# Six modulation row tiles multiplied on VectorE during the first feed-forward stage, and two more moved into the loop over recurrent heads

## The chip, the cores and the metric

The kernel runs on one core of a Trainium2 chip. Its time is the device time of one execution in microseconds (us), the median of three runs. Engines are named as the profile names them: PE is TensorE (PEld its weight loads), DVE is VectorE, ACT is ScalarE, POOL is GpSimd, SP is the queue that issues most DMAs.

## The reference, cut to what matters

Two transformer blocks follow each other, on 256 tokens of width 1024, all in fp32. What the change touches is the first block's conditioning: nine rows of 1024 numbers, computed once from a single vector `c`, that scale, shift and gate the three sub-blocks.

```
sc = silu(c)                                         # c: (1, 1024)
mod = sc @ ada_w + ada_b                             # ada_w: (1024, 9*1024)
(sh1, sc1, g1, sh2, sc2, g2, sh3, sc3, g3) = split(mod, 9)

y = rmsnorm(h, ffn1_pre_g) * (1 + sc1) + sh1
y = (silu(y @ w_gate) * (y @ w_up)) @ w_down         # 1024 -> 2816 -> 1024
h = h + 0.5 * g1 * rmsnorm(y, ffn1_post_g)
y = rmsnorm(h, mix_pre_g) * (1 + sc2) + sh2
y = token_mix(y, ...)                                # two recurrent mixers, 4 heads each
h = h + g2 * rmsnorm(y, mix_post_g)
...                                                  # second feed-forward with sh3, sc3, g3
...                                                  # second block: attention, RWKV, 16384 experts
```

## The kernel before

All large weights come through one ring in SBUF of four slots of 1 MB (a chunk is 128 partitions x 2048 fp32 numbers). SP issues the chunks in the order in which they are consumed. It may refill a slot when PE has begun the chunk after the one in it: `begun` counts the chunks that PE has begun, and chunk g is issued at `begun >= g - 2` (L2476).

The feed-forward matmuls are fp32 split in two: ACT casts a chunk to its rounded top (`top_chunk_act`, L342, two halves of 1024 columns), DVE subtracts the top in place to leave the rest (`rest_chunk_dve`, L353, two halves), and PE does three passes (L375 to L377). The first stage has 22 gate-and-up tiles (`staying_split_pe`, 48 matmuls with 256 columns each, one chunk each) and then 11 down chunks (`down_part`). After each gate-and-up tile ACT takes the silu (L856) and DVE multiplies and splits the result (L914, L369, L370). ACT may cast tile i+1 once PE has begun tile i, since the tops have two slots. DVE does, in program order, the rest of tile i+1 and then the product of tile i (`hidden_tile`).

The rows of `mod` come in 18 tiles of 512 columns, numbered 0 to 17. Each takes two chunks of `ada_w`. Tiles 0 to 3 are made before the stage. Tile t is made on PE in three steps: `ada_groups_pe` (L641, eight fp32 matmuls with 32 weight columns and 512 moving columns, four of them side by side in the array, then the bias, L650), a copy by ACT (L661), and `ada_sum_pe` (L657), a matmul with a matrix of ones that sums the partitions and spreads the result over all of them, evacuated by ACT (L665). Tiles 4 to 9, 14 and 15 are hosted in the first stage: behind every one of its first 16 gate-and-up tiles stands half of such a tile, and so its chunk stands in the ring. Tiles 10 and 11 stand behind the stage, 12 and 13 behind the loop over recurrent heads, 16 and 17 behind the mixer's output. `ada_rest_dve` (L724) scales rows SC2 (tiles 8, 9), SC3 (tiles 14, 15) and G1 (tiles 4, 5) in the down part.

The loop over recurrent heads (L1105 on, eight iterations) makes on PE the decays of the next step (L1071 to L1076), the attention matmuls of this one (`attend`, L1087) and the read-out of the last (L1098). ACT takes the exponentials (L1181), and DVE multiplies (L1302, L1304), masks (L1313) and reduces (L1320). ACT and DVE take each of them in the same order.

Of the kernel before, what the change touches and what calls it, by code (L numbers as in the profile page):

```python
# [14 lines left out]
ALU = mybir.AluOpType  # L15
# [8 lines left out]
S, D, F = 256, 1024, 2816  # L24
# [167 lines left out]
def program(nc, dram, out, where):  # L192

    ctx = ExitStack()
    with ctx:
# [373 lines left out]

        def staying_split_pe(pe, queue):  # L570

            bank = queue.take(pe)
            w = next_split_chunk(pe, KT)
            for j in range(2):
                for k in range(KT):
                    first, last = three_passes(pe, bank[:, j * S:(j + 1) * S].rearrange("p (t s) -> p t s", t=TT),
                                               [x[:, j * P:(j + 1) * P] for x in w[k]],
                                               (y_top[:, :, k, :], y_rest[:, :, k, :]), k == 0, k == KT - 1)
                    if j == 0 and k == 0:
                        first.then_inc(begun, 1)  # L580
            last.then_inc(queue.done, 1)
# [39 lines left out]
        ADA, ADA_FIRST = N_MOD * D // 512, 4  # L621
        HOSTED = [4, 5, 6, 7, 8, 9, 14, 15]
        BEHIND = {"ffn1": (10, 11), "scan": (12, 13), "mix": (16, 17)}

        def partial(tile):

            if tile < ADA_FIRST:
                return arena3[:, tile * 512:(tile + 1) * 512]
            if tile in HOSTED:
                return arena5[:, 7 * D - 512:7 * D]  # L630
            where, at = {10: (arena3, 2048), 12: (arena3, 4096), 16: (arena2, 0)}[tile - tile % 2]
            return where[:, at + tile % 2 * 512:at + tile % 2 * 512 + 512]

        def ada_groups_pe(pe, tile, halves=(0, 1)):
            if 0 in halves:
                ada_groups_pe.bank = A.take(pe)
            bank = ada_groups_pe.bank
            for c in halves:
                w = next_chunk(pe)[:, :].rearrange("p (k n) -> p k n", k=4)
                for k in range(4):  # L640
                    ins = pe.matmul(bank[32 * k:32 * k + 32, :], silu_c[:, 4 * c + k, :], w[:, k, :],  # L641
                                    start=(c == 0), stop=(c == 1 and k > 0))
                    if k == 0:
                        ins.then_inc(begun, 1)
            if 1 not in halves:
                return

            if tile in (0, ADA_FIRST):
                pe.wait_ge(sem(f"ada_b_in{int(tile > 0)}"), 16)
            pe.matmul(bank[0:32, :], ones_32, arena1[:, tile * 512:(tile + 1) * 512], start=False, stop=True  # L650
                      ).then_inc(A.done, 1)
# [72 lines left out]
        def ada_rest_dve(dve):  # L724

            await_mark(dve, "hosted_rows")
            dve.wait_ge(sem("gains_in"), 16)
            for i, sc in ((1, SC2), (2, SC3)):
                nc.vector.scalar_tensor_tensor(mod[:, sc, :], mod[:, sc, :], 1.0, gains[:, 2 * i, :], ALU.add, ALU.mult)
            nc.vector.scalar_tensor_tensor(mod[:, G1, :], mod[:, G1, :], 0.5, gains[:, 1, :], ALU.mult, ALU.mult  # L730
# [10 lines left out]

        split_at = [4 * ADA_FIRST // 2]
        for i in range(FT + FT // 2 - 1):
            split_at.append(split_at[-1] + 1 + (i < 2 * len(HOSTED)))

# [10 lines left out]
        def ffn_pe(pe, tag):  # L756
# [43 lines left out]
            for g in range(FT // 2 - 2):  # L800
                w = next_split_chunk(pe, 2)
                for t in range(TT):
                    first = down_part(w, g, t)
                    if t == 0:
                        first.then_inc(begun, 1)
            last_two = [next_split_chunk(pe, 2), next_split_chunk(pe, 2)]
# [34 lines left out]
        def ffn_act(act, tag):  # L841
# [17 lines left out]
            if tag == "ffn1":  # L859
                for g in range(FT // 2):  # L860
                    gate(2 * g, 0)
                    if 0 < g <= len(HOSTED):
                        ada_sum_act(act, HOSTED[g - 1])
                        if g == len(HOSTED):
                            mark("hosted_rows", A.free, 4 + A.emptied.n)
                    gate(2 * g + 1, 1)
                    if g < len(HOSTED):
                        ada_groups_act(act, HOSTED[g])
                for i in range(FT + 1, FT + FT // 2 - 1):
                    top_of_tile_act(act, i)  # L870
                act.wait_ge(sem("rows_scaled"), 1)
                top_chunk_act(act, 2)
# [23 lines left out]
        def ffn_dve(dve, tag, sc, sh, g):  # L896
# [29 lines left out]
            for i in range(1, FT // 2):  # L926
                if tag == "ffn1":
                    rest_of_tile_dve(dve, FT + i)
                    if i == 1:
                        ada_rest_dve(dve)  # L930
# [87 lines left out]
        def mix_pe(pe):  # L1018
# [86 lines left out]
            for i in range(HEADS * TT):  # L1105
# [14 lines left out]
        def mix_act(act):  # L1120
# [56 lines left out]
            for i in range(HEADS * TT):  # L1177
                e = decayed[i % 2][:, 0].rearrange("p l s -> p (l s)")
                for a0, b0 in ((0, 512), (512, NL * P)) + (((NL * P, NL * P + 2 * P),) if i % TT else ()):
                    bank = A.get(act)  # L1180
                    nc.scalar.activation(e[:, a0:b0], bank[:, 0:b0 - a0], ACT.Exp).then_inc(A.free, 1)  # L1181
                mark(f"decay{i}", A.free, 4 + A.emptied.n)
            act.wait_ge(sem("h_att"), HEADS * TT)
            act.dma_start(arena2[:, 3 * D:6 * D], dram["gains"][3 * D:6 * D].partition_broadcast(P)
# [13 lines left out]
        def mix_dve(dve):  # L1198
# [146 lines left out]
            for t in range(TT):  # L1345
# [3 lines left out]
                vec.tensor_tensor(yb[:, t, :], yb[:, t, :], mixg[:, t, :], ALU.mult).then_inc(sem("y_mixed"), 1)  # L1349
            late_gate_dve(dve, G2, 1.0, 3, "ffn1")  # L1350
            residual_dve(dve, 0, G2, BY_HALF, "ffn2")
            scaled_dve(0, SC3)
# [1101 lines left out]
        source = tile_at(range(ADA_FIRST))  # L2454
        for i in range(FT):
            source.append(ffn1_at[i])
            if i < 2 * len(HOSTED):
                source.append(tile_at(HOSTED)[i])
        source += ffn1_at[FT:] + tile_at(BEHIND["ffn1"])
        source += range(rest_at, rest_at + 16)  # L2460
        source += tile_at(BEHIND["scan"]) + list(range(rest_at + 16, rest_at + 20)) + tile_at(BEHIND["mix"])
        source += range(rest_at + 20, chunk_of["mix2"])
# [5 lines left out]
        def _(sp):  # L2468
# [135 lines left out]
```

## Time and profile before

| | |
|---|---|
| median of 3 runs | 1949.12 us (1948.37 to 1952.76) |
| the profiled execution | 1958.65 us, of which its span is 1956.8 us |
| busy in the span | PE 1811.9 us (93%), DVE 1139.4 (58%), ACT 768.4 (39%), POOL 334.8 (17%) |
| chain that ended last | PE 76%, DVE 9%, DMA 7%, ACT 4% |
| mean granted TensorE clock | 0.967 of full speed |
| DMA | 315.98 MB in the span, mean 161 GB/s |

The profiled execution lies 9.5 us above the median of the runs; durations come from it alone. Busy shares are means over stages with different limits, so a stage is read by its own window. A PE row's end is modelled: a matmul of 256 columns is shown as 0.28 us while the next starts 0.12 us after it. Starts are therefore what to subtract. The first stage's gate-and-up part runs from 53.58 to 225.65 us, its down part to 290.5, the mixer to about 530, of which the loop over recurrent heads is 431 to 480.

### The profile page before, as it was taken

To read this page: it belongs to the slowest core of one execution; us is meant where nothing else is said; L and a number is where in the kernel's file an instruction comes from. 1 tells how busy PE (TensorE), PEld (TensorE's weight loads), DVE (VectorE), ACT (ScalarE), POOL (GpSimd) and SP (SyncE) were. 2 spreads that over 40 slices of the span, in tenths; PEclk is the share of its full clock that TensorE was granted. 3 is DMA by queue.
4 is the path that set the end of the run, shared out by engine and by line. 5 is a ranking of instruction groups with operands and counts; after the bars stand their busy time and mean duration, and the time that the engine had idled before them with its cause. 6 is when DMAs were issued, how large, how long until landed. Compare 5 with 4: busy or idle time off the path is not lost.

```text
span 1956.8 us, 32839 instructions
## 1 busy us (share of the span) xinstructions
PE 1811.9 (93%) x12830; PEld 1557.4 (80%) x12830; DVE 1139.4 (58%) x1952; ACT 768.4 (39%) x1170; POOL 334.8 (17%) x314
## 2 busy tenths in 40 slices
PE   4999998987899999999878899999999999999997
PEld 1777877864399978976863798999999998888885
DVE  2443545759355544695443469958889964444444
ACT  2333344451345444552111443444444443333334
POOL 1000000000000000000000038760000025555553
PEclk8999997999999998999998899999999999999999
DMA  9566554521555553442003335554444456666664
GB/s 359 208 257 245 170 178 178 185 86 66 225 172 189 176 172 119 151 151 87 3 2 129 130 123 164 179 162 140 142 141 142 145 175 192 193 192 192 193 191 158
DMA packets 62080, 315.98 MB, mean 161 GB/s; under 512 B 6896, under 2 KB 7184, under 8 KB 40720
## 3 DMA queue, kind: packets, MB, share of 16 engines
q1 hardware_dynamic: 60768, 305.94, 46.8%
q10 hardware_dynamic: 1136, 8.39, 1.2%
q8 instruction: 85, 1.39, 0.3%
q14 instruction: 27, 0.22, 0.0%
q0 software_dynamic: 64, 0.04, 0.0%
HBM read 313.29 MB, written 1.05 MB: 161 GB/s over the span
## 4 chain that ended last, share of the span: by engine, by line
PE 76%; DVE 9%; DMA 7%; ACT 4%; POOL 2%; issue 2%; SPq 0%; POOLq 0%; DVEq 0%; ACTq 0%
PE bank L375 21%; PE bank L376 20%; PE bank L377 20%; DMA ring<-in_stream 4%; PE bank L590 3%; DMA ring<-in_experts 2%; PE bank L2127 2%; DVE ring_rounded L353 2%; POOL ring_rounded L2419 2%; PE bank L536 2%; ACT arena_rounded L342 1%; PE bank L641 1%; DVE field L1320 1%; ACT ring_rounded L2225 1%; PE bank L1549 1%
## 5 line engine op out<-in xcount | busy, mean ns | idle before, releaser
L377 PE MATMUL bank<-yb_rounded,ring_rounded 128*128 128x256 f32 x2080 | 595.3, 286 | 0.0
L377 PEld LDWEIGHTS bank<-yb_rounded,ring_rounded 128*128 128x128 f32 x2080 | 406.0, 195 | 0.0
L353 DVE TENSOR_TENSOR ring_rounded<-ring,arena_rounded 128x1024 fp32r<-128x1024 f32 x218 | 256.9, 1221 | 218.7 <-ACT arena_rounded L342 218.4
L2225 ACT CAST ring_rounded<-ring 128x1024 fp32r<-128x1024 f32 x250 | 262.6, 1051 | 279.1 <-DMA ring<-in_experts 279.1
L375 PE MATMUL bank<-yb_rounded,arena_rounded 128*128 128x256 f32 x1104 | 323.5, 293 | 24.1 <-POOL ring_rounded L831 10.2
L376 PE MATMUL bank<-yT_rounded,arena_rounded 128*128 128x256 f32 x1104 | 319.7, 290 | 0.0
L342 ACT CAST arena_rounded<-ring 128x1024 fp32r<-128x1024 f32 x222 | 221.3, 1047 | 191.3 <-PE bank L375 119.6
L375 PE MATMUL bank<-yb_rounded,ring_rounded 128*128 128x256 f32 x976 | 283.0, 290 | 10.3 <-POOL ring_rounded L2419 7.9
L376 PE MATMUL bank<-yT_rounded,ring_rounded 128*128 128x256 f32 x976 | 275.9, 283 | 0.0
L2378 DVE TENSOR_TENSOR ring_rounded<-ring,ring_rounded 128x1024 fp32r<-128x1024 f32 x128 | 156.9, 1226 | 191.6 <-ACT ring_rounded L2225 191.6
L376 PE MATMUL bank<-ring_rounded,arena_rounded 128*128 128x512 f32 x688 | 268.4, 390 | 0.0
L375 PEld LDWEIGHTS bank<-yb_rounded,arena_rounded 128*128 128x128 f32 x1104 | 219.8, 199 | 40.4 <-issue 20.9
L2419 POOL TENSOR_TENSOR ring_rounded<-ring,ring_rounded 128x1024 fp32r<-128x1024 f32 x46 | 126.4, 2762 | 647.5 <-ACT ring_rounded L2225 647.5
L376 PEld LDWEIGHTS bank<-yT_rounded,arena_rounded 128*128 128x128 f32 x1104 | 219.8, 199 | 0.2 <-issue 0.2
L375 PE MATMUL bank<-ring_rounded,arena_rounded 128*128 128x512 f32 x512 | 199.4, 389 | 1.1 <-POOL arena_rounded L2437 1.1
L377 PE MATMUL bank<-ring_rounded,arena_rounded 128*128 128x512 f32 x512 | 199.2, 389 | 0.0
L375 PEld LDWEIGHTS bank<-yb_rounded,ring_rounded 128*128 128x128 f32 x976 | 186.7, 191 | 13.5 <-ACT field L2236 7.2
L376 PEld LDWEIGHTS bank<-yT_rounded,ring_rounded 128*128 128x128 f32 x976 | 186.9, 192 | 0.1
L2434 POOL CAST arena_rounded<-field 128x256 fp32r (+1 forms) x128 | 94.2, 736 | 415.7 <-PE bank L375 415.7
L376 PEld LDWEIGHTS bank<-ring_rounded,arena_rounded 128*128 128x128 f32 x688 | 129.5, 188 | 26.7
L375 PEld LDWEIGHTS bank<-ring_rounded,arena_rounded 128*128 128x128 f32 x512 | 96.1, 188 | 21.7 <-DVE ring_rounded L2378 1.5
L377 PEld LDWEIGHTS bank<-ring_rounded,arena_rounded 128*128 128x128 f32 x512 | 96.1, 188 | 20.0
(389 smaller groups left out, 2606.1 us busy)
## 6 DMA issues: line engine op xcount, KB each, us to landing
ring<-in_stream SPq DMA_DIRECT2D x160, 1024.0 KB, 4.9
ring<-in_experts SPq DMA_DIRECT2D x256, 512.0 KB, 3.5
field<-in_gains ACTq DMA_DIRECT2D x1, 2560.0 KB, 8.9
const<-in_const SPq DMA_DIRECT2D x1, 1602.0 KB, 15.1
field<-in_gains ACTq DMA_DIRECT2D x1, 1536.0 KB, 6.7
xh<-in_x ACTq DMA_DIRECT2D x1, 1024.0 KB, 5.5
field<-in_norms ACTq DMA_DIRECT2D x1, 1024.0 KB, 10.3
field<-in_lns ACTq DMA_DIRECT2D x1, 1024.0 KB, 4.7
```

The source lines that it names most:

```text
L342: nc.scalar.copy(top, ring[:, g % SLOTS, half * HALF:(half + 1) * HALF]).then_inc(sem("weight_top_ready"), 1)
L353: ins = nc.vector.tensor_tensor(ring_r[:, g % SLOTS, half], ring[:, g % SLOTS, half], top.bitcast(F32), ALU.subtract)
L375: first = pe.matmul(bank, s_top, m_top, start=start, stop=False)
L376: pe.matmul(bank, s_top, m_rest, start=False, stop=False)
L377: return first, pe.matmul(bank, s_rest, m_top, start=False, stop=stop)
L536: ins = pe.matmul(two[t][:, :], src[:, c + k, t * P:(t + 1) * P], w[:, k, :], start=(c + k == 0), stop=(c + k == k_tiles - 1))
L590: ins = pe.matmul(four[2 * t + n][:, :], yT[:, c + k, t * P:(t + 1) * P], w[:, k, :], start=(c + k == 0), stop=(c + k == KT - 1))
L2127: ins = pe.matmul(bank[:, q * P:(q + 1) * P], hot[:, g % 2, 0, q, :], hot[:, g % 2, 1, q, :], start=True, stop=True)
L2225: nc.scalar.copy(expert_top[:, n % E_SLOTS, :], expert_w[:, n % E_SLOTS, :]).then_inc(expert_top_ready, 1)
L2378: vec.tensor_tensor(expert_rest[:, slot, :], expert_w[:, slot, :], expert_top[:, slot, :].bitcast(F32), ALU.subtract).then_inc(v_split, 1)
L2419: nc.gpsimd.tensor_tensor(expert_rest[:, slot, :], expert_w[:, slot, :], expert_top[:, slot, :].bitcast(F32), ALU.subtract).then_inc(u_spl ...
L2434: nc.gpsimd.tensor_copy(h_top[:, b, :], src).then_inc(h_top_ready, 1)
```

## The change

Tiles 4 to 9 leave `ada_groups_pe`. Their ring chunks, twelve, now stand behind gate-and-up tiles 1, 3, 5, ... 21 and behind the second down chunk (`ROW_BEHIND`, numbered 1 to 23 in the joint count of both parts), one for every second tile in place of one for every tile. In `row_part_dve` DVE adds each chunk to the row in place: four `scalar_tensor_tensor` of 128 x 512, row = w * silu(c) + row, with silu(c) as a scalar per partition. The row starts as zeros with the bias in partition 0, which the prologue had already put there. Each of the four waits for the one before it. PE's part is the matmul with ones alone (`row_sum_pe`, six of them, behind joint tiles 6, 10, 14, 18, 21 and 26), and ACT evacuates it. PE passes over the row chunk, and the next tile's first matmul counts two begun chunks. SP, before it refills the slot of a row chunk, also waits for `row_step`, DVE's count.

Tiles 14 and 15 go, unchanged in form, into the loop over recurrent heads: the groups in iterations 1 and 3, the sums in 2 and 4. The scaling of SC3 goes to DVE's work ahead of the mixer's residual, and `ada_rest_dve` from the first to the sixth step of the down part.

```diff
-        HOSTED = [4, 5, 6, 7, 8, 9, 14, 15]
+        HOSTED = [4, 5, 6, 7, 8, 9]
+        LOOPED = {1: 14, 3: 15}
...
+        row = lambda tile: arena1[:, tile * 512:(tile + 1) * 512]
+        ROW_BEHIND = [2 * h + 1 for h in range(2 * len(HOSTED))]
+        split_at, row_at = [2 * ADA_FIRST], []
...
+        SUM_BEHIND = {6: 4, 10: 5, 14: 6, 18: 7, FT - 1: 8, FT + 4: 9}
+
+        def row_part_dve(dve, i):
+
+            if i not in ROW_BEHIND:
+                return
+            h = ROW_BEHIND.index(i)
+            g, tile, c = row_at[h], HOSTED[h // 2], h % 2
+            if h == 0:
+                dve.wait_ge(sem("ada_b_in1"), 16)
+            dve.wait_ge(landed[g % SLOTS], 16 * (g // SLOTS + 1))
+            w = ring[:, g % SLOTS, :].rearrange("p (k n) -> p k n", k=4)
+            for k in range(4):
+                dve.wait_ge(sem("row_step"), 4 * h + k)
+                nc.vector.scalar_tensor_tensor(row(tile), w[:, k, :], col("c")[:, 4 * c + k:4 * c + k + 1], row(tile),
+                                               ALU.mult, ALU.add).then_inc(sem("row_step"), 1)
+
+        def row_sum_pe(pe, tile):
+
+            pe.wait_ge(sem("row_step"), 8 * (HOSTED.index(tile) + 1))
+            bank = A.take(pe)
+            pe.matmul(bank[:, :], cst("ones"), row(tile), start=True, stop=True).then_inc(A.done, 1)
...
-                for g in range(FT // 2):
-                    gate_up_tile(2 * g, 0)
-                    if 0 < g <= len(HOSTED):
-                        ada_sum_pe(pe, HOSTED[g - 1])
-                    if g < len(HOSTED):
-                        ada_groups_pe(pe, HOSTED[g], (0,))
-                    gate_up_tile(2 * g + 1, 1)
-                    if g < len(HOSTED):
-                        ada_groups_pe(pe, HOSTED[g], (1,))
+                for i in range(FT):
+                    staying_split_pe(pe, V, 1 + (i - 1 in ROW_BEHIND))
+                    if i in SUM_BEHIND:
+                        row_sum_pe(pe, SUM_BEHIND[i])
+                    if i in ROW_BEHIND:
+                        chunks.n += 1
...
             def hidden_tile(i, j):
                 if tag == "ffn1":
                     rest_of_tile_dve(dve, i + 1)
+                    row_part_dve(dve, i)
...
                 if i:
                     read_out(i - 1)
+                if i in LOOPED:
+                    ada_groups_pe(pe, LOOPED[i])
+                if i - 1 in LOOPED:
+                    ada_sum_pe(pe, LOOPED[i - 1], but=3)
...
                 sp.wait_ge(begun, g - 2)
+                if g - SLOTS in row_at:
+                    sp.wait_ge(sem("row_step"), 4 * (row_at.index(g - SLOTS) + 1))
                 sp.dma_start(ring[:, g % SLOTS, :], stream[source[g]]).then_inc(landed[g % SLOTS], 16)
```

The order of the instructions shows it at three places. First PE at the end of an even gate-and-up tile, before: the sum of one row tile and half the groups of the next stand between the last matmul of the tile and the first of the next.

```order
L375 MATMUL bank<-yb_rounded,arena_rounded 128x256
L376 MATMUL bank<-yT_rounded,arena_rounded 128x256
L377 MATMUL bank<-yb_rounded,ring_rounded 128x256
L657 MATMUL bank<-field,const 128x512
L641 MATMUL bank<-ring,tiny 32x512 x4
L375 MATMUL bank<-yb_rounded,arena_rounded 128x256
```

The same engine now, at the end of tile 6, the first that has anything behind it (L769 is the new sum):

```order
L375 MATMUL bank<-yb_rounded,arena_rounded 128x256
L376 MATMUL bank<-yT_rounded,arena_rounded 128x256
L377 MATMUL bank<-yb_rounded,ring_rounded 128x256
L769 MATMUL bank<-field,const 128x512
L375 MATMUL bank<-yb_rounded,arena_rounded 128x256
```

Four such places are left in the 22 gate-and-up tiles, and one behind the last of them; at all the others one tile follows the other directly.

Second DVE in the gate-and-up tiles, before (L353 is the rest of the next tile, L914 to L370 the product of this one):

```order
L353 TENSOR_TENSOR ring_rounded<-ring,arena_rounded 128x1024 [waits weight_top_ready] x2
L914 TENSOR_TENSOR field<-field,bank 128x256 [waits gate_ready,dve_bank_filled]
L369 CAST arena_rounded<-field 128x256 [waits dve_step]
L370 TENSOR_TENSOR arena_rounded<-field,arena_rounded 128x256 [waits dve_step]
```

and now, from the product of tile 0 to that of tile 1 and the rest of tile 3 (L944 is the old L914, L762 the new multiply-adds):

```order
L944 TENSOR_TENSOR field<-field,bank 128x256 [waits gate_ready,dve_bank_filled]
L369 CAST arena_rounded<-field 128x256 [waits dve_step]
L370 TENSOR_TENSOR arena_rounded<-field,arena_rounded 128x256 [waits dve_step]
L353 TENSOR_TENSOR ring_rounded<-ring,arena_rounded 128x1024 [waits weight_top_ready] x2
L762 SCALAR_TENSOR_TENSOR field<-ring,cols,field 128x512 [waits row_step,chunk_landed2,ada_b_in1]
L762 SCALAR_TENSOR_TENSOR field<-ring,cols,field 128x512 [waits row_step] x3
L944 TENSOR_TENSOR field<-field,bank 128x256 [waits gate_ready,dve_bank_filled]
```

In every second tile the four multiply-adds now stand between the rest of the next tile and the product of this one.

Third PE in the loop over recurrent heads, iterations 1 to 2, before (L1071 to L1076 decays, L1087 attention, L1098 read-out):

```order
L1087 MATMUL bank<-field 128x128 x8
L1091 MATMUL bank<-field 128x128
L1098 MATMUL bank<-field 128x128
L1071 MATMUL bank<-const,field 128x512
L1071 MATMUL bank<-const,field 128x384
L1075 MATMUL bank<-const,field 128x128
L1076 MATMUL bank<-const,field 128x128
L1087 MATMUL bank<-field 128x128 x8
```

and now (the lines are 31 further down, L640 and L649 are the groups and their bias):

```order
L1118 MATMUL bank<-field 128x128 x8
L1122 MATMUL bank<-field 128x128
L1129 MATMUL bank<-field 128x128
L640 MATMUL bank<-ring,tiny 32x512 x8
L649 MATMUL bank<-field,tiny 32x512
L1102 MATMUL bank<-const,field 128x512
L1102 MATMUL bank<-const,field 128x384
```

The groups of tile 14 now stand ahead of the decays of step 3, and those of tile 15 in the same way ahead of the decays of step 5.

## Rows read from the trace of the kernel before

**Rows 1.** Busy by stretch: PE, PEld, DVE, ACT, POOL, then PEclk, DMA share, GB/s.

```profile
160.00:181.20 21.20, 18.31 (x120) 15.08 (x116) 6.95 (x11) 5.72 (x8) 0.00 (x0) 0.84 0.59 199
...
437.00:480.00 43.00, 31.56 (x183) 24.09 (x183) 42.19 (x52) 7.54 (x15) 0.00 (x0) 0.96 0.00 1
```

**Rows 2.** Waits of PE, 53 to 228 us: total, times, longest.

```profile
PE bank L375 <- DVE ring_rounded L353: 7.9, 8, 2.9
```

**Rows 3.** Timeline of PE, tiles 1 to 3: start, duration, engine, line.

```profile
61.20 1.07 PE L641 MATMUL bank<-ring,tiny 128*32 128x512 f32 x8
62.20 0.38 PE L375 MATMUL bank<-yb_rounded,arena_rounded 128*128 128x256 f32 x1
...
68.14 1.07 PE L641 MATMUL bank<-ring,tiny 128*32 128x512 f32 x8
...
70.58 0.36 PE L375 MATMUL bank<-yb_rounded,arena_rounded 128*128 128x256 f32 x1 [0.54 <-DVE ring_rounded L353]
...
76.41 1.02 PE L657 MATMUL bank<-field,const 128*128 128x512 f32 x2
...
78.36 0.39 PE L375 MATMUL bank<-yb_rounded,arena_rounded 128*128 128x256 f32 x1
```

**Rows 4.** Timeline of PE, first gate-and-up tile and first down chunk.

```profile
53.58 0.58 PE L375 MATMUL bank<-yb_rounded,arena_rounded 128*128 128x256 f32 x1 [2.00 <-DVE yT_rounded L518]
...
227.76 0.48 PE L375 MATMUL bank<-arena_rounded 128*128 128x512 f32 x1 [2.11 <-DVE small L925]
```

**Rows 5.** Timeline of ACT, silu of tiles 16, 17 and 21.

```profile
196.04 0.38 ACT L856 ACTIVATE field<-bank 128x256 f32<-128x256 f32 x1 [4.47 <-PE bank L377]
...
202.65 0.38 ACT L856 ACTIVATE field<-bank 128x256 f32<-128x256 f32 x1 [3.26 <-PE bank L377]
...
225.69 0.38 ACT L856 ACTIVATE field<-bank 128x256 f32<-128x256 f32 x1 [3.49 <-PE bank L377]
```

**Rows 6.** Timeline of all engines, chunk of tile 2: cast, rest, product.

```profile
67.00 2.00 ACT L342 CAST arena_rounded<-ring 128x1024 fp32r<-128x1024 f32 x2 [5.30 <-DMA ring<-in_stream]
...
68.08 2.36 DVE L353 TENSOR_TENSOR ring_rounded<-ring,arena_rounded 128x1024 fp32r<-128x1024 f32 x2 [5.08 <-ACT arena_rounded L342]
...
70.35 0.41 DVE L914 TENSOR_TENSOR field<-field,bank 128x256 f32<-128x256 f32 x1
...
71.13 0.43 DVE L370 TENSOR_TENSOR arena_rounded<-field,arena_rounded 128x256 fp32r<-128x256 f32 x1
```

**Rows 7.** Groups of DVE, 0 to 300 us: count, busy us, mean ns, idle before.

```profile
L428 DVE SCALAR_TENSOR_TENSOR yb<-xh,small,field 128x1024 f32<-128x1024 f32 x4 | 5.1, 1285 | 0.1
...
L444 DVE SCALAR_TENSOR_TENSOR yb<-bank,small,field 128x512 f32<-128x512 f32 x4 | 2.8, 745 | 0.1
```

**Rows 8.** DMA issues in windows 60:160, 160:175 and 197:226: count, size, us to landing.

```profile
ring<-in_stream SPq DMA_DIRECT2D x24, 1024.0 KB, 5.7
...
ring<-in_stream SPq DMA_DIRECT2D x4, 1024.0 KB, 7.3
...
ring<-in_stream SPq DMA_DIRECT2D x5, 1024.0 KB, 4.8
```

**Rows 9.** Timeline of PE, groups of tile 16 behind the mixer's output.

```profile
523.08 1.92 PE L641 MATMUL bank<-ring,tiny 128*32 128x512 f32 x16
...
525.87 1.07 PE L641 MATMUL bank<-ring,tiny 128*32 128x512 f32 x8
```

**Rows 10.** Timeline of ACT in the loop over heads: exponentials of steps 3 and 5.

```profile
442.52 1.47 ACT L1181 ACTIVATE field<-bank 128x512 f32<-128x512 f32 x3 [2.94 <-PE bank L1071]
...
454.42 1.47 ACT L1181 ACTIVATE field<-bank 128x512 f32<-128x512 f32 x3 [4.95 <-PE bank L1071]
```

**Rows 11.** Timeline of DVE: products of steps 3 and 5, first residual.

```profile
446.91 1.22 DVE L1302 TENSOR_TENSOR field<-field 128x1024 f32<-128x1024 f32 x1
...
458.62 1.22 DVE L1302 TENSOR_TENSOR field<-field 128x1024 f32<-128x1024 f32 x1
...
517.76 0.16 DVE L438 RECIPROCAL small<-small 128x1 f32<-128x1 f32 x1 [23.09 <-ACT small L408]
```

More of the change, by code:

```diff
@@ L579, in staying_split_pe @@
                     if j == 0 and k == 0:
-                        first.then_inc(begun, 1)
+                        first.then_inc(begun, begins)
             last.then_inc(queue.done, 1)
@@ L628, in partial @@
                 return arena3[:, tile * 512:(tile + 1) * 512]
-            if tile in HOSTED:
-                return arena5[:, 7 * D - 512:7 * D]
-            where, at = {10: (arena3, 2048), 12: (arena3, 4096), 16: (arena2, 0)}[tile - tile % 2]
+            where, at = {10: (arena3, 2048), 12: (arena3, 4096), 14: (arena3, 3072), 16: (arena2, 0)}[tile - tile % 2]
             return where[:, at + tile % 2 * 512:at + tile % 2 * 512 + 512]
@@ L727, in ada_rest_dve @@
             dve.wait_ge(sem("gains_in"), 16)
-            for i, sc in ((1, SC2), (2, SC3)):
-                nc.vector.scalar_tensor_tensor(mod[:, sc, :], mod[:, sc, :], 1.0, gains[:, 2 * i, :], ALU.add, ALU.mult)
+            nc.vector.scalar_tensor_tensor(mod[:, SC2, :], mod[:, SC2, :], 1.0, gains[:, 2, :], ALU.add, ALU.mult)
             nc.vector.scalar_tensor_tensor(mod[:, G1, :], mod[:, G1, :], 0.5, gains[:, 1, :], ALU.mult, ALU.mult
@@ L738, in late_gate_dve, with row_sum_act @@
             v(nc.vector.scalar_tensor_tensor(mod[:, g, :], mod[:, g, :], weight, gains[:, gain, :], ALU.mult, ALU.mult))
-        split_at = [4 * ADA_FIRST // 2]
-        for i in range(FT + FT // 2 - 1):
-            split_at.append(split_at[-1] + 1 + (i < 2 * len(HOSTED)))
+        row = lambda tile: arena1[:, tile * 512:(tile + 1) * 512]
+        ROW_BEHIND = [2 * h + 1 for h in range(2 * len(HOSTED))]
+        split_at, row_at = [2 * ADA_FIRST], []
+        for i in range(FT + FT // 2):
+            if i in ROW_BEHIND:
+                row_at.append(split_at[-1] + 1)
+            split_at.append(split_at[-1] + 1 + (i in ROW_BEHIND))
+        split_at.pop()
+        SUM_BEHIND = {6: 4, 10: 5, 14: 6, 18: 7, FT - 1: 8, FT + 4: 9}
[16 more added lines that the diff above has]
+            pe.matmul(bank[:, :], cst("ones"), row(tile), start=True, stop=True).then_inc(A.done, 1)
+        def row_sum_act(act, tile):
+            bank = A.get(act)
+            nc.scalar.copy(row(tile), bank[:, :]).then_inc(A.free, 1)
         def top_of_tile_act(act, i):
@@ L804, in ffn_pe @@
                     if t == 0:
-                        first.then_inc(begun, 1)
+                        first.then_inc(begun, 1 + (tag == "ffn1" and FT + g - 1 in ROW_BEHIND))
+                if tag == "ffn1" and FT + g in SUM_BEHIND:
+                    row_sum_pe(pe, SUM_BEHIND[FT + g])
+                if tag == "ffn1" and FT + g in ROW_BEHIND:
+                    chunks.n += 1
             last_two = [next_split_chunk(pe, 2), next_split_chunk(pe, 2)]
@@ L859, in ffn_act @@
             if tag == "ffn1":
[L860 to L868, printed above, removed]
+                for i in range(FT):
+                    gate(i, i)
+                    if i in SUM_BEHIND:
+                        row_sum_act(act, SUM_BEHIND[i])
                 for i in range(FT + 1, FT + FT // 2 - 1):
                     top_of_tile_act(act, i)
+                    if i - 2 >= FT and i - 2 in SUM_BEHIND:
+                        row_sum_act(act, SUM_BEHIND[i - 2])
+                        mark("hosted_rows", A.free, 4 + A.emptied.n)
                 act.wait_ge(sem("rows_scaled"), 1)
@@ L1182, in mix_act @@
                 mark(f"decay{i}", A.free, 4 + A.emptied.n)
+                if i - 1 in LOOPED:
+                    ada_groups_act(act, LOOPED[i - 1])
+                if i - 2 in LOOPED:
+                    ada_sum_act(act, LOOPED[i - 2])
+                    mark("looped_rows", A.free, 4 + A.emptied.n)
             act.wait_ge(sem("h_att"), HEADS * TT)
@@ L1350, in mix_dve @@
             late_gate_dve(dve, G2, 1.0, 3, "ffn1")
+            await_mark(dve, "looped_rows")
+            v(nc.vector.scalar_tensor_tensor(mod[:, SC3, :], mod[:, SC3, :], 1.0, gains[:, 4, :], ALU.add, ALU.mult))
             residual_dve(dve, 0, G2, BY_HALF, "ffn2")
```

20 lines of the change are left out of this document (11 added, 9 removed).

## Prediction

> **What bounds the kernel now.** I read the page's shares first (PE busy 93% of the span), then the stretches, the waits of PE in the first feed-forward stage, and the timeline of one pair of tiles there. In that stage PE is the engine that ends last. From 53 to 228 us it waited only 7.9 us for the rest of a chunk [rows 2]. One pair of tiles, from 62.20 to 78.36, takes 16.16 us [rows 3]. Free tiles go faster: the silus of tiles 17 and 21 start at 202.65 and 225.69, four tiles in 23.04, so 5.76 us a tile and 11.52 a pair [rows 5]. The missing 4.6 us are what is hosted: half the groups (61.20 to 62.20, 1.0), the other half with the bias and a wait of 0.54 (68.14 to 70.58, 2.4), and the sum (76.41 on). So PE is bound by its own program, a quarter of which here is row tiles at 32 weight columns. In the loop over heads it is the other way round: DVE is busy 42.2 of 43.0 us and PE 31.6 [rows 1].
>
> **The gate-and-up part.** Eight pairs carry hosted work, three don't. Tile 0 takes 7.6 us (53.58 to 61.20) [rows 3, 4], because it starts at the lower clock; that stays. Then 21 tiles at 5.76 are 121.0 us. A sum that stands alone between two tiles costs 0.85: silu 16 to silu 17 is 6.61 us with the sum of tile 15 between them, against 5.76 [rows 5]. Four sums inside the part are 3.4 us. For the first pairs, in which the chunks are not yet in step, I add 1 us of waiting. Sum: 7.6 + 121.0 + 3.4 + 1.0 = 133.0 us. Before it was 172.1 (53.58 until just ahead of the silu at 225.69) [rows 4, 5]. **Gain 39.1 us**, if PE still ends last.
>
> Does it? DVE gets 48 multiply-adds, four per pair. The trace has none from ring and row with a scalar per partition at 512 columns. The nearest are L444, same form and size from a bank, 745 ns, and L428, 1024 columns from SBUF, 1285 ns, an upper bound [rows 7]. The lower bound is half of L428, 0.64. I take 0.75, and 0.04 for the wait on the step before, as the gap between the chained L914 and L370 shows: 3.16 us per pair. DVE's work per pair is then two rests (2.36 each), two products (1.2 each, 70.35 to 71.56) and 3.16, that is 10.3 us of 11.5 [rows 6]. It fits in sum. The order matters more, since there is a new cycle. The slot of a row chunk is refilled with the next even tile's chunk, and SP waits for DVE's fourth step. Around the cycle: landing 4.8 us [rows 8], from the start of the cast to the end of the rest 3.44 (67.00 to 70.44) [rows 6], 3.16 for the four steps, and some 0.2 for SP and semaphores: 11.6 us a pair. PE needs 11.52 and, with a sum in every second pair, 11.95 on average. So the cycle lies just under PE's own time, and PE's slack grows by 0.35 a pair. I take PE as the bound and nothing more for the cycle; its bound from above is the third rival's price. The row chunk itself has a whole tile longer to land than it needs, and three chunks in 11.5 us are 273 GB/s, where the part's five undisturbed ones and the pairs before show landings of 4.8 and 5.7 [rows 8].
>
> **The turn to the down part.** The last gate-and-up tile (21) has a row part ahead of its product, with nothing behind it that hides it. Its chunk (tile 22's) lands about 1.4 us into tile 21, by the cycle above; rest 3.44, steps 3.16, product 1.2 and 0.4 to the first down matmul are 9.6 us after the tile's start, when the tile's own matmuls have ended at 5.9. The gap is 3.7 to 3.8 us instead of 2.11 [rows 4]: **loss 1.7**. The sum behind tile 21 lies inside it. The one behind joint tile 26 costs 0.85 in the down part: **loss 0.85**. There DVE has 2.4 us of rest per chunk against PE's 5.7 (227.76 [rows 4] to 290.5 in eleven chunks), so the last row part and `ada_rest_dve` cost nothing; without that cover they would be 3.2 and 2.4.
>
> **Tiles 14 and 15 in the loop over heads.** One tile of groups with its bias is 2.79 us of PE (523.08 to 525.87) [rows 9]. It delays the decays that stand behind it. Queued behind them are ACT's exponentials, then DVE's product. For step 3 ACT ended at 443.99 and DVE began at 446.91 [rows 10, 11]: 2.9 us of cover, enough. PE idles 11.4 of 43.0 us over the loop's eight iterations [rows 1], 1.4 each, so two iterations take in 2.9 of the 2.79 and 0.85 (sum of tile 14), and 0.8 is carried on. Tile 15 adds 2.79: step 5's exponentials are 3.55 late against a cover of 458.62 less 455.89, 2.73 [rows 10, 11]. **Loss 0.8.** Bounds: 0 (all covered) and 7.3 (both tiles and both sums laid on the path). Their ring chunks were prefetched long before, since the ring is idle there (1 GB/s [rows 1]). The scaling of SC3 (1.22 us) moves into the 23.1 us in which DVE waits for the mixer's output [rows 11]: nothing. ACT loses eight copies where it was never late: nothing.
>
> **Sum.** -39.1 + 1.7 + 0.85 + 0.8 = -35.7 us, so the profiled execution, 1958.65 us, becomes 1922.9. But one of its pairs, tiles 13 to 14 in 160.00 to 181.20, took 21.2 us and not 16.2: four chunks took 7.3 us to land there, and the granted clock fell to a mean of 0.84 [rows 1, 8]. Nothing in the program is special in that place, so 5 of the 35.7 may be an accident of this execution, which lies 9.5 us above the median. Against the median, 1949.12, the gain is 30.7 without it and 35.7 with it. I take 31: **1918 us**.
>
> **Rivals.**
> *The chunk cycle ends last.* For it speaks that it lies at 11.6 against 11.95, so that any term that grows shows at once. When one chunk is issued close behind another, as the row chunk and the even tile's are, landing took longer: 5.7 in the paired windows, 7.3 in the bad one [rows 8]. Against it: DVE's steps hold the second issue back by two to three us, so the first has nearly landed. With 6.5 us of landing the cycle is 13.3, 1.35 over PE, in 11 pairs 15 us: 1933. With 0.9 instead of 0.79 per step, another 0.4 a pair.
> The Trainium skill (DMA: Bandwidth & Descriptors, "Latency and other measured facts") says that the memory's own access time rises from 0.2 us to 2 us under high load. By that rule the landing grows with the third chunk per pair, which would make it about 6 us and this rival likely; the trace's 4.8 alone and 5.7 in pairs point the same way, though the second is mostly queueing behind the first [rows 8].
> The same case grows if PE's clock drops in the gaps. The trace shows it once: PE waited behind tile 13, and the clock's mean in the stretch was 0.84 [rows 1].
> The Trainium skill (TensorE: Matmul & The Clock Gate, "HAM oscillation — how this bites in real kernels") says that waits for a DMA put the array back to the half clock, again at every wait that recurs. By it each late pair could cost some us more. In rows 3 PE waited 0.54 in a pair and the next tiles ran on at 0.12 us a matmul, so waits of that size don't do it here.
>
> *The loop over heads takes the moved tiles in full.* The bound of 7.3 instead of 0.8: 1924.5. For it: PE's idle time there is cut in pieces under 1.5 us. Against: DVE's two numbers of cover above.
>
> *Slower than before.* VectorE's steps are the mechanism, in the gate-and-up part. If four of them hold the cycle, PE, SP and the next chunk all wait on them, and the pair is 8.44 + 4 steps. The gain of 31 is spent over 11 pairs at 2.8 us a pair, so at a pair of 14.8 and a step of 1.58 us; at a step of 1.8 the time is 1959. Against it: twice the columns take 1.285 us [rows 7], and POOL, which could disturb DVE, has nothing to do until the mixer. Only contention between the ring's landings and DVE's reads could do it, and L353 reads the same ring at 1.22 for 1024 columns under the same load.
>
> *The change doesn't do what it says*, no difference: PE is free of the groups but waits as long as they took. That is a cycle of exactly the old 16.2 us a pair less the down part's loss, a special case of the last two, and no row speaks for it.
>
> **How the numbers follow.** Forecast with its own spread 1911 to 1926 (with and without the 5 us, cycle 0.5 a pair over PE): 0.62. Chunk cycle, 1926 to 1940: 0.28. Loop over heads in full: 0.05, inside or just above the forecast's spread. Slower by VectorE's steps: 0.03. No difference: 0.02. What a measurement of this kernel can tell from no change is 0.2%, 4 us. Faster 0.95, same 0.02, slower 0.03. The range that leaves out 2 in 10: 1909 to 1935.
>
> **What would show it.** Right, if in the new profile L641's successor is gone from the gate-and-up part, silus come 5.8 us apart with 6.6 at a sum, the multiply-adds show 0.75 us, PE's waits for the rest (L353) stay under 5 us in the part, the gap ahead of the first down chunk is near 4 us, and the loop over heads is 0 to 2 us longer. The chunk cycle shows as waits of PE for L353 at every even tile, with ACT in front of it waiting for the ring's DMA. Wrong altogether, if the first down matmul starts later than 205 us instead of near 191.

## The result, and the profile after

| | before | changed |
|---|---|---|
| median of 4 runs | 1948.74 us (1948.15 to 1952.76) | 1918.05 us (1916.6 to 1921.22) |
| ratio | | 0.9837, 95% interval 0.9819 to 0.9855 |
| span of the profiled execution | 1956.8 us | 1915.0 us |

The change makes the kernel 30.7 us faster. The forecast was 1918; how far that is merit and how far luck is told below.

What answers to the waits and the durations of before [rows 2, 7]. First the waits of PE in the changed kernel from 50 to 193 us (total, times, longest), then those of ACT from 60 to 187, then the group of the new multiply-adds (count, busy us, mean ns, idle before), then the DMA issues from 60 to 187 and the one issued at 177.4.

```profile
PE bank L375 <- DVE small L955: 4.5, 1, 4.5
PE bank L375 <- DVE yT_rounded L518: 2.0, 1, 2.0
PE bank L375 <- DVE ring_rounded L353: 1.4, 4, 0.5
```

```profile
ACT arena_rounded L342 <- DMA ring<-in_stream: 15.5, 10, 2.8
```

```profile
L762 DVE SCALAR_TENSOR_TENSOR field<-ring,cols,field 128x512 f32<-128x512 f32 x48 | 36.0, 751 | 1.3
```

```profile
ring<-in_stream SPq DMA_DIRECT2D x31, 1024.0 KB, 5.3
...
ring<-in_stream SPq DMA_DIRECT2D x1, 1024.0 KB, 6.8
```

PE waits 1.4 us for rests in 22 tiles, where it had waited 7.9 us and had had the groups to do besides. A multiply-add takes 751 ns. A chunk now lands in 5.3 us at the median, with three per pair of tiles; it was 4.8 alone and 5.7 with four per pair [rows 8]. The ten chunks that refill the slot of a row chunk, those of the even tiles 4 to 20 and of tile 22, took longer, 5.25 to 6.8 us and 5.8 on average. All ten casts of them waited for the DMA: those are the ten waits of ACT above.

The silus of tiles 6 to 9 in ACT's timeline answer to [rows 5]:

```profile
95.42 0.38 ACT L887 ACTIVATE field<-bank 128x256 f32<-128x256 f32 x1 [3.49 <-PE bank L377]
...
97.39 2.00 ACT L342 CAST arena_rounded<-ring 128x1024 fp32r<-128x1024 f32 x2 [0.53 <-DMA ring<-in_stream]
102.02 0.38 ACT L887 ACTIVATE field<-bank 128x256 f32<-128x256 f32 x1 [2.63 <-PE bank L377]
...
107.78 0.38 ACT L887 ACTIVATE field<-bank 128x256 f32<-128x256 f32 x1 [3.49 <-PE bank L377]
110.43 2.00 ACT L342 CAST arena_rounded<-ring 128x1024 fp32r<-128x1024 f32 x2 [2.27 <-DMA ring<-in_stream]
113.54 0.38 ACT L887 ACTIVATE field<-bank 128x256 f32<-128x256 f32 x1 [1.10 <-PE bank L377]
114.47 2.00 ACT L342 CAST arena_rounded<-ring 128x1024 fp32r<-128x1024 f32 x2 [0.55 <-PE bank L375]
```

Three intervals, 6.60 (with a sum in it), 5.76 and 5.76. The cast at 110.43 had waited 2.27 us for its chunk; that is the chunk cycle, close to late. In 5 of 21 intervals it is late by 0.4 to 0.7 us, in a sixth by 0.1, together 2.8 us. From the issue of one such refill to that of the next is 12.16 us on average (80.17 to 177.44 us, eight rounds), where PE alone needs 11.95 a pair.

The turn to the down part, in the changed kernel's DVE timeline and in PE's row that answers to the second of [rows 4]:

```profile
181.55 0.42 DVE L944 TENSOR_TENSOR field<-field,bank 128x256 f32<-128x256 f32 x1 [0.79 <-ACT field L887]
...
185.32 2.36 DVE L353 TENSOR_TENSOR ring_rounded<-ring,arena_rounded 128x1024 fp32r<-128x1024 f32 x2 [2.56 <-ACT arena_rounded L342]
187.60 3.11 DVE L762 SCALAR_TENSOR_TENSOR field<-ring,cols,field 128x512 f32<-128x512 f32 x4
190.62 0.41 DVE L944 TENSOR_TENSOR field<-field,bank 128x256 f32<-128x256 f32 x1
```

```profile
192.20 0.77 PE L375 MATMUL bank<-arena_rounded 128*128 128x512 f32 x1 [4.46 <-DVE small L955]
```

Tile 21's matmuls ended at 186.88 (its silu starts at 186.92). Its product starts 3.7 us later, because DVE was at the rest of tile 22 and then at the row part. From there to 192.20 PE did only one sum.

In the loop over heads, ACT's exponentials of steps 3 and 5 in the changed kernel, and DVE's products behind them, answer to [rows 10, 11]:

```profile
407.18 1.47 ACT L1216 ACTIVATE field<-bank 128x512 f32<-128x512 f32 x3 [0.47 <-PE bank L1102]
...
418.08 0.58 ACT L660 COPY field<-bank 128x512 f32<-128x512 f32 x1 [4.73 <-PE bank L649]
419.14 1.47 ACT L1216 ACTIVATE field<-bank 128x512 f32<-128x512 f32 x3 [0.47 <-PE bank L1102]
```

```profile
408.70 1.22 DVE L1342 TENSOR_TENSOR field<-field 128x1024 f32<-128x1024 f32 x1
...
420.28 0.29 DVE L1367 COPY yb<-bank 128x128 f32<-128x128 f32 x1
420.64 1.23 DVE L1342 TENSOR_TENSOR field<-field 128x1024 f32<-128x1024 f32 x1
```

The exponentials of step 5 end at 420.61 and the product starts at 420.64: they are just late, by 0.2 us. Those of step 3 are just in time.

### The profile page after: what moved, and what is told of

It is laid out like the page before. It is cut to its first block, busy times and chain, and to the rows that moved or that the text cites. A ratio compares the mean times of both kernels' runs of the same rounds, so it can differ in the third digit from the quotient of the medians.

```text
span 1915.0 us, 32685 instructions
## 1 busy us (share of the span) xinstructions
PE 1783.7 (93%) x12722; PEld 1550.6 (81%) x12722; DVE 1178.7 (62%) x2000; ACT 765.0 (40%) x1164; POOL 337.1 (18%) x314
## 4 chain that ended last, share of the span: by engine, by line
PE 77%; DVE 9%; DMA 6%; ACT 4%; POOL 2%; issue 2%; SPq 0%; DVEq 0%; POOLq 0%; ACTq 0%
PE bank L375 20%; PE bank L376 20%; PE bank L377 20%; DMA ring<-in_stream 5%; PE bank L590 3%; PE bank L2169 3%; DVE ring_rounded L353 2%; DVE field L762 2%; PE bank L536 2%; POOL ring_rounded L2461 1%; ACT arena_rounded L342 1%; DMA ring<-in_experts 1%; PE bank L2143 1%; PE bank L640 1%; PE bank L1591 1%
## 5 line engine op out<-in xcount | busy, mean ns | idle before, releaser
L353 DVE TENSOR_TENSOR ring_rounded<-ring,arena_rounded 128x1024 fp32r<-128x1024 f32 x218 | 256.9, 1221 | 161.8 <-ACT arena_rounded L342 161.4
L375 PE MATMUL bank<-yb_rounded,arena_rounded 128*128 128x256 f32 x1104 | 322.0, 292 | 15.9 <-POOL ring_rounded L862 8.3
L375 PE MATMUL bank<-yb_rounded,ring_rounded 128*128 128x256 f32 x976 | 283.1, 290 | 7.9 <-POOL ring_rounded L2461 6.5
L375 PEld LDWEIGHTS bank<-yb_rounded,arena_rounded 128*128 128x128 f32 x1104 | 218.6, 198 | 20.3 <-DVE yT_rounded L518 11.3
L375 PE MATMUL bank<-ring_rounded,arena_rounded 128*128 128x512 f32 x512 | 199.3, 389 | 0.8 <-POOL arena_rounded L2479 0.8
L375 PEld LDWEIGHTS bank<-yb_rounded,ring_rounded 128*128 128x128 f32 x976 | 186.7, 191 | 10.0 <-ACT field L2278 5.2
L2476 POOL CAST arena_rounded<-field 128x256 fp32r (+1 forms) x128 | 101.0, 789 | 407.6 <-PE bank L375 407.6
L375 PEld LDWEIGHTS bank<-ring_rounded,arena_rounded 128*128 128x128 f32 x512 | 96.1, 188 | 21.4 <-issue 1.2
```

The lines of the kernel that those rows point to most:

```text
L353: ins = nc.vector.tensor_tensor(ring_r[:, g % SLOTS, half], ring[:, g % SLOTS, half], top.bitcast(F32), ALU.subtract)
L375: first = pe.matmul(bank, s_top, m_top, start=start, stop=False)
L2476: nc.gpsimd.tensor_copy(h_top[:, b, :], src).then_inc(h_top_ready, 1)
```

## The experiments

A stage table stands behind them, read from the starts of matmuls in each trace.

**Tiles 14 and 15 moved, nothing else.** The kernel before with the loop's part of the change.

```diff
-        HOSTED = [4, 5, 6, 7, 8, 9, 14, 15]
+        HOSTED = [4, 5, 6, 7, 8, 9]
+        LOOPED = {1: 14, 3: 15}
```

> The kernel before with only tiles 14 and 15 moved into the loop over heads; tiles 4 to 9 stay hosted on PE. My theory (PE's program order is the price in the gate-and-up part, and the loop has cover): two hosted pairs of tiles go from 16.2 to 11.5 us, -9.3, the loop over heads gets 0.3 longer, so 1948.7 - 9.0 = 1939.7 us. Rival (the loop takes the moved tiles in full, 7.3): 1947. The profile also shows whether a pair of 21 us with a lower clock stands in the gate-and-up part again; if it is an accident of the one execution of before, all hosted pairs are near 16.2.

Measured: 1934.86 us (4 runs, 1932.32 to 1940.2) against 1950.91 of before, ratio 0.9928 (0.9907 to 0.9949): -14.0 us by the ratio and -16.0 by these medians, where -9.0 was expected. The rival's 1947 is out. The stage itself did what was said: the gate-and-up part with its turn takes 160.6 us where two other traces of the kernel before have 169.5 and 168.8, so -8.6. The loop took 0.3 more. The other 5 to 6 us lie outside the stages touched: see the stage table.

**The multiply-adds left out.**

```diff
-            for k in range(4):
-                dve.wait_ge(sem("row_step"), 4 * h + k)
-                nc.vector.scalar_tensor_tensor(row(tile), ...).then_inc(sem("row_step"), 1)
+            dve.sem_inc(sem("row_step"), 4)
```

> The changed kernel without the 48 multiply-adds (the chunks are still loaded and DVE still releases them; the rows of tiles 4 to 9 are left without their products, so that part of the computation is missing). Theory (the steps cost little in the 22 tiles, through the chunk cycle at 11.6 to 12.1 us a pair, and 3 us at the turn to the down part): the waits of PE for the rest go (2 us), the turn falls from 5.2 to 2.1 us, and 0.6 of lower clock behind it: 1918.1 - 5.5 = 1912.5. Rival (the chunk cycle costs nothing, only the turn does): 1914.5. Rival (the steps disturb ACT, PE or the DMAs beyond their order): under 1908.

Measured: 1913.51 us (1910.51 to 1916.07), ratio 0.9818 (0.9802 to 0.9834). All 21 intervals between silus are 5.76, or 6.61 with a sum. So 5.76 a tile and 0.85 a sum are what PE needs. The 48 multiply-adds, 36 us of DVE, cost 4.5 us of the kernel's time by the medians and 3.7 by the ratios, whose intervals overlap, so that the totals can't tell the theory (1912.5) from the first rival (1914.5); only the second rival (under 1908) is out. The stages can: the gate-and-up part with its turn takes 135.4 instead of 140.8 us, which is the 2.8 us of late intervals and 2.9 at the turn, less 0.3 in tile 0, and the down part 61.9 instead of 63.3.

**The multiply-adds twice.**

```diff
-            for k in range(4):
-                dve.wait_ge(sem("row_step"), 4 * h + k)
-                nc.vector.scalar_tensor_tensor(row(tile), w[:, k, :], ...
+            for k in range(8):
+                dve.wait_ge(sem("row_step"), 8 * h + k)
+                to = row(tile) if k % 2 else arena5[:, 7 * D - 512:7 * D]
+                nc.vector.scalar_tensor_tensor(to, w[:, k // 2, :], ...
```

> The changed kernel with each multiply-add done twice, the first time into a scratch tile: eight steps of 0.75 us per row chunk in one chain, SP and PE wait for the last. Theory (a cycle of landing, cast, rest, steps and refill): the pair goes from 12.1 to 11.6 + 3.2 = 14.8 us, 11 pairs +30, the turn +3.1: 1951, slower than before. Rival (no cycle, only DVE's busy time counts, 13.5 us a pair): 11 pairs +15, turn +3: 1937. Rival (DVE is hidden in the pairs): turn alone, 1921.

Measured: 1947.88 us (10 runs, 1943.01 to 1954.26), ratio 0.999 (0.9975 to 1.0006). The whole gain is gone, though the kernel isn't slower than before, as 1951 had said. This settles the cycle against the two rivals (1937 and 1921). ACT's timeline of one pair:

```profile
149.37 2.00 ACT L342 CAST arena_rounded<-ring 128x1024 fp32r<-128x1024 f32 x2 [4.10 <-DMA ring<-in_stream]
154.00 0.38 ACT L888 ACTIVATE field<-bank 128x256 f32<-128x256 f32 x1 [2.63 <-PE bank L377]
...
159.76 0.39 ACT L888 ACTIVATE field<-bank 128x256 f32<-128x256 f32 x1 [3.50 <-PE bank L377]
...
163.95 1.99 ACT L342 CAST arena_rounded<-ring 128x1024 fp32r<-128x1024 f32 x2 [2.74 <-DMA ring<-in_stream]
170.03 0.38 ACT L888 ACTIVATE field<-bank 128x256 f32<-128x256 f32 x1 [4.08 <-PE bank L377]
```

From cast to cast of the even tiles 14.58 us (14.55 to 14.86 over nine pairs), where the sum of the cycle's terms gave 14.8. Both casts wait for the DMA, not for PE: what is late is the refill of the row chunk's slot. Odd tiles' intervals stay at 5.76.

**The row part ahead of the rest.**

```diff
-                    rest_of_tile_dve(dve, i + 1)
                     row_part_dve(dve, i)
+                    rest_of_tile_dve(dve, i + 1)
```

> The changed kernel with the row part ahead of the rest of the next tile in DVE's order (it was behind it). DVE waited there for the cast, 1.6 to 2.6 us per pair, while the row chunk had landed. Theory: the cycle loses the cast and the rest (3.4 us) and no longer binds, the turn to the down part falls by 2.5 us as the row part of tile 21 fills DVE's wait: waits for the rest -1.4 to -2, turn -2.5, clock -0.6: 1918.1 - 4.5 = 1913.5. Rival (the row chunk lands later than the rest's top is ready, so the row part delays the rest by up to 3.1 us in each pair): slower than the changed kernel, up to 1930.

Measured: 1925.67 us (4 runs, 1921.75 to 1926.86), ratio 0.9869 (0.9853 to 0.9886), 6 us slower than the changed kernel by the ratios. My theory fell, the rival held. PE's waits in the variant, and DVE's timeline of one pair:

```profile
PE bank L375 <- DVE ring_rounded L353: 10.8, 10, 1.4
```

```profile
166.39 0.42 DVE L944 TENSOR_TENSOR field<-field,bank 128x256 f32<-128x256 f32 x1 [2.62 <-ACT field L887]
...
167.52 3.11 DVE L762 SCALAR_TENSOR_TENSOR field<-ring,cols,field 128x512 f32<-128x512 f32 x4
170.55 2.35 DVE L353 TENSOR_TENSOR ring_rounded<-ring,arena_rounded 128x1024 fp32r<-128x1024 f32 x2
```

DVE's idle time had stood ahead of the rest only because the chunk was late there. With the slot free earlier the chunk lands earlier against PE: its cast starts at 167.57, so its rest could have started some 1.1 us later, as in [rows 6], at 168.6. The row part stands ahead of it until 170.55. The rest ends 6.5 us after the product of the tile before starts, and a tile is 5.76. Ten waits of 1.1 us on average are the price; the turn did fall (1.9 instead of 4.5 us of waiting).

**Both last row chunks into the down part.** So that tile 21 has none.

```diff
-        ROW_BEHIND = [2 * h + 1 for h in range(2 * len(HOSTED))]
+        ROW_BEHIND = [2 * h + 1 for h in range(2 * len(HOSTED) - 2)] + [FT + 1, FT + 3]
-        SUM_BEHIND = {6: 4, 10: 5, 14: 6, 18: 7, FT - 1: 8, FT + 4: 9}
+        SUM_BEHIND = {6: 4, 10: 5, 14: 6, 18: 7, FT - 1: 8, FT + 6: 9}
...
-                    if i == 6:
+                    if i == 8:
                         ada_rest_dve(dve)
```

> The changed kernel with the last two row chunks behind joint tiles 23 and 25 in place of 21 and 23, so that no multiply-adds stand ahead of the product of the last gate-and-up tile; the sum of tile 9 goes to joint tile 28 and the scaling of the rows to the eighth step of the down part. Theory (the steps and the late chunk of tile 22 make the turn 5.2 us long, where 2.1 is left without them, and the lower clock behind it 0.6): 3.7 us less than the changed kernel, beside which it runs here. Rival (the down part pays it back, since two row chunks now stand among its chunks and its cycle of landing, cast, rest and steps is longer than its 5.5 us of PE): the gain of the turn is lost by waits of PE in the first down chunks, the same as the changed kernel within 1 us.

Measured, beside the changed kernel: 1915.09 us (5 runs, 1911.49 to 1918.46), ratio 0.9815 (0.9802 to 0.9829). Its PE waits from 51 to 225 us:

```profile
PE bank L375 <- DVE ring_rounded L353: 2.0, 4, 0.7
PE bank L375 <- DVE yT_rounded L518: 2.0, 1, 2.0
PE bank L375 <- DVE small L955: 1.2, 1, 1.2
```

The wait at the turn is 1.2 instead of 4.5 us, the down part takes 62.0 instead of 63.3 and 63.7, and has one of the four waits for the rest, 0.4 us: next to nothing is paid back. It beats the kernel before clearly. Against the changed one it is 4.9 us of medians with intervals that overlap, so the total leaves it open; the two stages together take 198.7 us where two traces of the changed kernel have 204.1 and 206.0.

**The changed kernel again.**

> The changed kernel once more, to stand beside the variant on the same chip, and for a second trace. By the first four runs 1918 against 1949 of before, ratio 0.9837. The second trace also shows which of the differences outside the stages touched (prologue -2.2, mixer's projections -2.5, second block -3.5 us) stay; if they are accidents of one execution they change, if they are effects of the change they stay.

Measured: 1920.01 us (5 runs, 1913.64 to 1925.46), ratio 0.9843 (0.9822 to 0.9865).

**Two more traces of the kernel before.**

> The kernel before once more, one look, for the pair of gate-and-up tiles 13 and 14 that took 21.2 us. If that was an accident of the one execution, as I took it in the forecast, all eight hosted pairs are near 16.2 us here, the gate-and-up part is 167 and not 172 us. If it is part of the program (a place in its own instruction or data stream), it stands again at tiles 13 and 14, and then moving tiles 14 and 15 off the stage, which alone gave 16 us where 9 were expected, takes it away.

> The same once more: with two looks an accident that hits one in a few executions is told from one that comes each time. Accident: no pair over 17 us in at least one of the two. Part of the program: over 20 us at tiles 13 and 14 in both.

Measured: 1948.03 and 1949.49 us. No pair of tiles is over 17 us in either. The stretch that took PE 18.3 busy us at a mean clock of 0.84 in the first trace [rows 1] reads in these two:

```profile
160.00:181.20 21.20, 20.20 (x156) 16.72 (x153) 7.30 (x11) 5.84 (x8) 0.00 (x0) 1.00 0.70 253
```

```profile
160.00:181.20 21.20, 20.65 (x161) 16.87 (x154) 7.44 (x12) 6.10 (x9) 0.00 (x0) 1.00 0.70 252
```

So the pair of 21.2 us was an accident of one execution. What made its four chunks land in 5.6 to 9.1 us (7.3 at the median [rows 8]) stays open.

Stages in us, read from the starts of matmuls. The down column ends at the start of its last L375, the projections begin with the turn (L496) behind it. Two stretches stand in no column: 8.6 to 10.4 us between these two, and 558.4 to 563.1 us between the output turn and the second block's experts. The last column is the mean granted clock in the projections.

| trace | to tile 0 | gate-and-up and turn | down | projections | loop over heads to output turn | second block's experts, to the end | clock in the projections |
|---|---|---|---|---|---|---|---|
| before | 53.6 | 174.2 | 61.9 | 131.0 | 61.5 | 905.2 | 0.91 |
| before again | 53.6 | 169.5 | 61.9 | 127.1 | 61.6 | 904.6 | 0.94 |
| before, third | 54.1 | 168.8 | 60.3 | 132.6 | 61.7 | 902.5 | 0.90 |
| changed | 51.4 | 140.8 | 63.3 | 128.5 | 61.9 | 901.6 | 0.92 |
| changed again | 52.0 | 142.3 | 63.7 | 124.7 | 63.4 | 905.5 | 0.96 |
| tiles 14, 15 only | 51.8 | 160.6 | 60.3 | 124.7 | 61.7 | 904.9 | 0.96 |
| no multiply-adds | 52.3 | 135.4 | 61.9 | 124.7 | 61.5 | 904.1 | 0.96 |
| multiply-adds twice | 52.5 | 166.6 | 65.7 | 128.5 | 63.3 | 901.5 | 0.92 |
| row part first | 52.0 | 148.7 | 62.8 | 128.4 | 61.9 | 904.1 | 0.93 |
| last two chunks moved | 52.0 | 136.7 | 62.0 | 131.3 | 61.6 | 905.4 | 0.91 |

## Why the prediction was right, and where it was not

*PE is bound by its program in the gate-and-up part: right.* The groups gone, tiles come at 5.76 us, a sum costs 0.85. In the changed kernel PE shares that place with the chunk cycle, as the next term shows.

*The accident of 5 us in the profile: right.* I had treated these 5 us as a chance of that execution and left them out of the gain; the two further traces of the kernel before don't have them. The four chunks of which the prediction says that they took 7.3 us took 7.1, 9.1, 7.5 and 5.6.

*The gate-and-up part, 133.0 us: it took 135.5, and 137.1 in the second trace.* The term that was too small is the waiting, 1 us in my sum: it is 2.8, and 4.8 in the second trace. The chunk cycle, which I took as lying just under PE's time (11.6 against 11.95), takes 12.16, because the refill lands in 5.8 us on average and not in 4.8; [rows 8] had 5.7 for chunks issued close behind others, and I had used the number for a chunk alone. Of the 2.8 us, the waits that the profile shows for the rest are 1.4. Tile 0 took 8.4 and not 7.6 us: it starts 2 us earlier, and more of it lies in the low clock (a mean of 0.68 over the tile, 0.75 before). The first rival's mechanism (the chunk cycle, which the working calls the third) thus acts, at 2.8 of its 15 us. With the steps doubled it decides, at 14.6 us a pair against 14.8 worked out.

*The turn, 3.75 us of gap: it was 5.3.* The mechanism was right, and one term off: tile 22's chunk landed 3 us into tile 21 and not 1.4. It was issued 2 us behind the row chunk of tile 21 and took 6.8 us. Moving that row chunk brings the gap back to 2.1 us, what it was before the change.

*The down part, +0.85: it was some +2.4.* The rest is the clock: in the changed kernel the 6 us around the turn have PE 1.5 us busy, and the granted clock's mean there is 0.74:

```profile
51.40:187.00 135.60, 134.04 (x1065) 131.11 (x1066) 102.52 (x147) 53.85 (x71) 0.00 (x0) 0.98 0.69 248
187.00:193.00 6.00, 1.54 (x4) 0.74 (x3) 4.71 (x9) 0.89 (x2) 0.00 (x0) 0.74 0.01 4
```

The first down matmuls then start 0.43 us apart and not 0.22. Two traces of the kernel before had this too, at their own turn, but for some 3 us, and the third not at all (it has the 60.3); the changed one has it for 4.5 us from the first down matmul, and for 5.4 in its second trace. The gap cost its own length and some of the work behind it, a step that my sum had not. The variant with the gap of 2.1 us has the full clock there and a down part of 62.0.
By the Trainium skill (TensorE: Matmul & The Clock Gate, "HAM oscillation — how this bites in real kernels") an idle stretch puts the array back to half its clock. Here the trace agrees for the 4.5 us of waiting at the turn (0.50 from 192.20 to 196.70), and not for the waits of 0.5 us in the tiles, behind which the stretch to 187 shows a clock of 0.98, its low part being that of tile 0.

*The loop over heads, +0.8: +0.3.* From the start of the first product of 1024 columns to the end of the last reduction it is 44.3 us in all three traces of the kernel before, and 44.5 to 44.6 in all seven of kernels with the two tiles moved; the 63.4 and 63.3 of two rows in the table thus lie outside it. The delay sits where it was put, at step 5, but is 0.2 there. The term that was too large is what is carried on from the first tile: the exponentials of step 5 are 2.9 us later against DVE than before, just as those of step 3 (2.9), where the sum had 3.55. So PE had taken up all of tile 14's groups and sum by then, and not only twice the mean idle time of 1.4.

*The multiply-adds, 0.75 us: 0.751.*

*That the total came out within a microsecond is luck.* Without the accident my terms sum to -30.7. Measured by stage, the mean of the two changed traces against the two undisturbed ones of before: gate-and-up with its turn -27.6 (I had -32.4), down +2.4, loop 0.3. That makes -25, and the runs show -30.7: my stages were nearly 6 us too good, and others made up for it. The rest lies in stages that the change doesn't touch, above all the prologue (-2.1) and the mixer's projections (-3.3).
The projections spread from 124.7 to 132.6 us, also between executions of one kernel (127.1 to 132.6 of before, 124.7 and 128.5 of the changed), and the spread goes with the granted clock, 0.96 where they take 124.7 and 0.90 where they take 132.6. So a few us there are chance. This also is why the first experiment gave 14 us for 9.
The prologue is 1.1 to 2.7 us shorter in every kernel in which tiles 14 and 15 are moved, seven traces against three. PE's rows show where. The last groups ahead of the stage and their bias, in the second trace of the kernel before and in the changed one:

```profile
33.59 1.94 PE L641 MATMUL bank<-ring,tiny 128*32 128x512 f32 x8 [1.45 <-DMA ring<-in_stream]
35.30 1.84 PE L650 MATMUL bank<-field,tiny 128*32 128x512 f32 x2
```

```profile
33.04 1.07 PE L640 MATMUL bank<-ring,tiny 128*32 128x512 f32 x8 [1.25 <-DMA ring<-in_stream]
33.93 1.02 PE L649 MATMUL bank<-field,tiny 128*32 128x512 f32 x2
```

From 33 to 37 us the granted clock is 0.57 or 0.58 in the three traces of the kernel before and 1.00 in the seven others. Why it falls there in the one program and not in the other, and so whether the 2 us belong to the change, stays open.

## What to carry to other kernels

When a step moves from a full engine to one with room, sum the room first, then look for the cycle that the move closes: here landing, cast, rest, four steps, refill, with one slot in it. Its length against the bound engine's period says whether the move is free, and doubling the step tests it in one run. Take each term from rows in which it stands in the same company: the landing of a chunk behind another one, not of a chunk alone. Idle time of an engine ahead of an instruction isn't free to be filled if it is there because that instruction's input is late for the same reason that you mean to remove.

## What the runs showed of the hardware

- Behind a wait of PE of 4.5 us the granted clock fell to the lower level (a mean of 0.74 over 187 to 193 us), and through ten waits of 1.1 us on average (the row part ahead of the rest) it stayed up (1.00 over 60 to 200 us). In between the length of the wait alone doesn't decide. With the multiply-adds doubled there are ten waits of 0.6 to 3.1 us. The clock fell behind three of them, of 2.2, 2.8 and 1.9 us (means of 0.56, 0.62 and 0.64 over the 3.5 to 4.3 us behind), and stayed at 1.00 behind the longest. At the turn it was down behind a wait of 2.1 us in two traces of the kernel before and up in the third. The mean with the multiply-adds doubled over 52.5 to 219 us was 0.95 (the column behind the engines' busy times), little under the 0.98 of the changed kernel's part:

```profile
52.50:219.00 166.50, 140.31 (x1066) 135.27 (x1067) 139.36 (x199) 54.28 (x72) 0.00 (x0) 0.95 0.60 202
```

- A 1 MB chunk landed in 4.8 us alone, in 5.3 us at the median with three per pair of tiles, and in 5.3 to 6.8 us when issued 1.2 to 2.6 us behind another.
- One execution of the kernel before had four chunks in a row with 5.6 to 9.1 us of landing, 7.3 at the median, with 5 us lost; the two other traces had no such pair of tiles.
- With a scalar per partition, a `scalar_tensor_tensor` of 128 x 512 in fp32 took 751 ns, and chained by a semaphore four of them started 0.79 us apart (187.60 to 190.71 us for the four).
- The stretch of the projections, the same program in all ten traces, took 124.7 us at a mean granted clock of 0.96 and 132.6 at 0.90: one trace isn't enough to size a term of a few us there.
